# A mixture-of-experts trunk: expert outputs added to the tokens by TensorE, block turns on VectorE

## What is computed

```python
expert_id = g_sel[:, None] * EXPERTS_PER_GROUP + top_i     # top-1 group, top-2 experts in it
...
def expert_block(args):
    xb, e = args
    hid = jax.nn.silu(xb @ w1[e]) * (xb @ w3[e])
    return hid @ w2[e]

ys = lax.map(expert_block, (xs, block_e)).reshape(n_rows, D)
ys = ys * w_buf[:, None].astype(ys.dtype)
out = jnp.zeros((T + 1, D), ys.dtype).at[tok_buf].add(ys)[:T]
```

## Time and profile before

| | us |
|---|---|
| median of 3 runs (lowest, highest) | 1711.97 (1709.97, 1712.51) |
| the profiled execution's own time | 1715.51 |
| its span, from the first to the last instruction | 1713.8 |

### The profile page before, as it was taken

How to read it: one execution, slowest core, us unless ns; L and a number is a source line. 1 busy time by engine, 2 the same in 40 slices (tenths; PEclk the granted TensorE clock), 3 DMA queues, 4 the chain that set the end, 5 groups by cost and what they waited for, 6 DMA issues and landing times.

```text
span 1713.8 us, 39713 instructions
## 1 busy us (share of the span) xinstructions
PE 1489.0 (87%) x16229; PEld 1002.4 (58%) x16230; DVE 588.4 (34%) x1383; ACT 342.5 (20%) x669; POOL 38.5 (2%) x68
## 2 busy tenths in 40 slices
PE   8999999997997999864999989989989999866673
PEld 7888888654554555532887844468555556433342
DVE  5347632422221222213634356733222222211113
ACT  5441313200000000001432334524100000000000
POOL 3000000000000000002000000000000000000001
PEclk9999999999999999987998999989999999988887
DMA  5621226799999999998212122055999997999995
GB/s 203 221 98 56 93 97 245 284 420 423 425 421 423 421 424 421 421 422 335 75 51 99 50 98 75 25 196 220 368 422 424 423 411 312 401 418 422 421 421 180
DMA packets 100998, 487.04 MB, mean 284 GB/s; under 512 B 10736, under 2 KB 22896, under 8 KB 84304
## 3 DMA queue, kind: packets, MB, share of 16 engines
q1 hardware_dynamic: 76544, 457.19, 65.5%
q10 hardware_dynamic: 20528, 17.10, 3.1%
q0 software_dynamic: 3872, 11.98, 2.2%
HBM read 467.58 MB, written 18.64 MB: 284 GB/s over the span
## 4 chain that ended last, share of the span: by engine, by line
issue 51%; DMA 24%; PE 21%; DVE 1%; ACTq 1%; POOL 1%; SPq 0%; POOLq 0%; ACT 0%; DVEq 0%
DMA EB<-in_m_w 17%; DMA y_rows<-SCR 5%; PE ps L1174 5%; PE ps L1176 5%; PE ps L1175 5%; PE ps L1304 2%; ACTq L623 1%; PE ps L1384 1%; DMA EB<-y_rows,pos_i 1%; PE ps L1319 1%; PE ps L1286 1%; DVE X L939 1%; POOL EB L484 1%; PE ps L1170 0%; DMA gain<-in_a_norm 0%
## 5 line engine op out<-in xcount | busy, mean ns | idle before, releaser
L1304 PE MATMUL ps<-EB,SCR 128*32 128x256 f32 x6016 | 386.9, 414 | 119.8 <-DMA EB<-in_m_w 93.2
L1304 PEld LDWEIGHTS ps<-EB,SCR 128*32 128x32 f32 x6016 | 221.5, 119 | 277.6 <-issue 191.7
L896 DVE TENSOR_TENSOR SCR<-SCR,ps 64x256 f32<-64x256 f32 x94 | 39.7, 423 | 616.1 <-ACT SCR L611 616.1
L1176 PE MATMUL ps<-EB_r 128*128 128x512 f32 x512 | 201.0, 393 | 0.0
L1319 PE MATMUL ps<-EB,SCR 128*32 128x256 f32 x3008 | 184.0, 385 | 1.3 <-issue 0.3
L1286 PE MATMUL ps<-H,SCR 128*32 128x256 f32 x3072 | 184.3, 379 | 0.0
L616 ACT ACTIVATE SCR<-ps 128x256 f32 (+1 forms) x94 | 36.1, 384 | 560.1 <-issue 374.6
L1286 PEld LDWEIGHTS ps<-H,SCR 128*32 128x32 f32 x3072 | 107.3, 110 | 58.2
L1319 PEld LDWEIGHTS ps<-EB,SCR 128*32 128x32 f32 x3008 | 105.6, 110 | 53.5 <-issue 18.4
L1174 PE MATMUL ps<-EB_r,H_r 128*128 128x512 f32 x320 | 127.4, 398 | 1.0 <-DVE EB L972 1.0
L1175 PE MATMUL ps<-EB_r,H_r 128*128 128x512 f32 x320 | 125.4, 392 | 0.0
(11 more groups left out here) (218 smaller groups left out, 1389.9 us busy)
## 6 DMA issues: line engine op xcount, KB each, us to landing
EB<-in_m_w SPq DMA_DIRECT2D x192, 2048.0 KB, 10.1
EB<-in_a_w_in SPq DMA_DIRECT2D x8, 2048.0 KB, 9.4
y_rows<-SCR ACTq DMA_DIRECT2D x376, 32.0 KB, 5.9
EB<-in_a_w_out SPq DMA_DIRECT2D x4, 2048.0 KB, 7.7
EB<-in_kv_w SPq DMA_DIRECT2D x4, 2048.0 KB, 14.2
EB<-in_b_w_qg SPq DMA_DIRECT2D x4, 2048.0 KB, 8.0
y_rows<-X SPq DMA_DIRECT2D x2, 2048.0 KB, 15.9
SCR<-ncum_rows ACTq DMA_DIRECT2D x16, 256.0 KB, 3.7
```

Source lines behind the costliest of these rows:

```text
L896: v.tensor_tensor(hid[0:HALF, :], silu[HALF:P, :], ps[0][HALF:P, 0:CW], ALU.mult).then_inc(m["hid"], 1)
L1176: return mm(o, left[1], right[0], start=False, stop=stop)
L1304: last = mm(ps[0][g * CAP:(g + 1) * CAP, 0:CW], xT[:, k, :], w[:, k, g % 2 * CW:(g % 2 + 1) * CW], start=k == 0, stop=k == KD - 1)
```

## The change

`y_rows`, its stores, `gather_outputs` and `combine` are gone. In their place:

- ACT copies the down products of item n, times the weight of each slot (`slot_w`), into `y_parts` as fp32r; DVE writes the rest (exact value minus the rounded one) as a second fp32r part. Two items are kept.
- `spread_tokens` on DVE builds 0/1 matrices of 32 x 256 for each of the four partition groups, from the rows of positions `pos_row`: which of 256 tokens each slot of two items belongs to.
- `move` on PE multiplies these with `y_parts`: 32 products of 32 rows of contraction, 128 tokens and 256 columns of output, in the four row groups of the array, each group into its own PSUM bank. In iteration n it handles the items n-1 and n-2 and one half of the tokens (`n & 1`), and it stands behind `gather(n + 1)`. DVE then adds two blocks of 1024 columns to `X`. After the loop two more `move`s handle what is left.
- The transposes of `hid` and of the gathered rows are gone from PE: DVE turns them in blocks of 32 x 32 (`v.transpose`), for which w1 and w3 are read with other columns side by side, and the rows of w2 are laid out as `(p c) n` instead of `(c p) n`.
- Before the loop there are new steps: the rows of positions by PE (8 products), `slot_hot` and `item_hot` on DVE, `slot_w` by PE (32 products) and ACT.
- The start of the keys and values of layer 0 is reordered: the split of its first weight tile now stands among the norms of the blocks.

The diff, cut to its core:

```diff
@@ moe_act @@
-                act.wait_ge(y_filled, 16 * ((Y_ROWS - SLOTS) // T))
-                item_silu(0)
-                item_output(0)
-                with act.Fori(1, total) as n:
-                    item_silu(n)
-                    store_before(n)
-                    item_output(n)
-                store_before(total)
...
+                act.wait_ge(slot_w_done, 2 * l + 1)
+                a.activation(slot_w, ps[6][:, 0:MAX_ITEMS], ACT.Copy).then_inc(slot_w_done, 1)
+                act.wait_ge(slot_w_done, 2 * l + 2)
+                with act.Fori(0, total) as n:
                     act.wait_ge(m["up"], n + 1)
+                    a.activation(silu, ps[0][:, 0:P], ACT.Silu).then_inc(m["silu"], 1)
                     act.wait_ge(m["down"], n + 1)
+                    a.activation(y_parts[:, bass.ds(n & 1, 1), 0, :], ps[2][:, CW:2 * CW].unsqueeze(1), ACT.Copy,
+                                 scale=slot_w[:, bass.ds(n, 1)]).then_inc(m["y_hi"], 1)
@@ moe_dve @@
+                def turn_item(n):
+                    dve.wait_ge(m["gath"], n + 1)
+                    v.transpose(xg.rearrange("p k c -> p (k c)"), ps[1][:, 0:CW]).then_inc(m["xg"], 1)
+                    dve.wait_ge(m["xg"], n + 1)
+                    v.tensor_tensor(xT, xg, gpk[:, l, :].unsqueeze(2).to_broadcast([P, KD, CAP]), ALU.mult)\
+                        .then_inc(m["xT"], 1)
+
+                def spread_tokens(dst, which, items, link, ready):
+                    toks = [pos_row[:, k, bass.ds(which * 2 * P, 2 * P)] for k in range(2)]
+                    for i in range(2):
+                        link(v.tensor_scalar(dst[:, i, :], toks[0], item_slot[:, bass.ds(items[i] + 2, 1)], None,
+                                             ALU.is_equal), i)
+                    for i in range(2):
+                        v.scalar_tensor_tensor(dst[:, i, :], toks[1], item_slot[:, bass.ds(items[i] + 2, 1)],
+                                               dst[:, i, :].bitcast(F32), ALU.is_equal, ALU.add).then_inc(ready, 1)
...
                 with dve.Fori(0, total) as n:
                     dve.wait_ge(m["silu"], n + 1)
-                    v.tensor_tensor(hid[0:HALF, :], silu[HALF:P, :], ps[0][HALF:P, 0:CW], ALU.mult).then_inc(m["hid"], 1)
-                    item_rows(n + 1)
-                    dve.wait_ge(m["hidT_tr"], n + 1)
-                    v.tensor_copy(hidT.rearrange("p (h j) c -> p j h c", h=2),
-                                  ps[2][:, 0:2 * P].rearrange("p (j c) -> p j c", j=2)[:, :, 0:HALF]
-                                  .rearrange("p j (h c) -> p j h c", h=2)).then_inc(m["hidT"], 1)
-                    item_xT(n + 1)
+                    v.tensor_tensor(hid.rearrange("p (c r) -> p r c", c=KE), silu.rearrange("p (r c) -> p r c", c=KE),
+                                    ps[0][:, P:2 * P].rearrange("p (r c) -> p r c", c=KE), ALU.mult).then_inc(m["hid"], 1)
+                    dve.wait_ge(m["hid"], n + 1)
+                    v.transpose(hidT.rearrange("p k c -> p (k c)"), hid).then_inc(m["hidT"], 1)
+                    turn_item(n + 1)
+                    dve.wait_ge(m["moved"], n + 1)
+                    for t in range(2):
+                        X_t = X[:, bass.ds((n & 1) * 2 + t, 1), :].rearrange("p a (g n) -> p (a g) n", g=CG)
+                        add = v.tensor_tensor(X_t, X_t, moved[1][:, :, t, :], ALU.add)
+                    add.then_inc(m["added"], 1)
...
+                    spread_tokens(spread, (n + 1) & 1, (n - 1 + ((n + 1) & 1), n - 1 + (n & 1)),
+                                  lambda ins, i: link(ins, i + 1), m["spread"])
+
+                    dve.wait_ge(m["y_hi"], n + 2)
+                    v.scalar_tensor_tensor(y_parts[:, bass.ds(n & 1, 1), 1, :], ps[2][:, CW:2 * CW].unsqueeze(1),
+                                           slot_w[:, bass.ds(n, 1)], y_parts[:, bass.ds(n & 1, 1), 0, :].bitcast(F32),
+                                           ALU.mult, ALU.subtract).then_inc(m["y_lo"], 1)
+                    select(n + 2, m, 0, lambda ins, k: link(ins, k + 2))
+                spread_tokens(spread, 1, (total - (total & 1), total - 2 + ((total + 1) & 1)), lambda ins, i: then(ins),
+                              end_spread)
@@ moe_pe @@
+                def move(banks, sides):
+                    for t in range(2):
+                        for i in range(2):
+                            for k in range(2):
+                                for g in range(CG):
+                                    rows = slice(g * CAP, (g + 1) * CAP)
+                                    last = mm(moved[banks][:, g, t, :], sides[rows, i, t * P:(t + 1) * P],
+                                              y_parts[rows, i, k, :], start=i == 0 and k == 0, stop=i == 1 and k == 1)
...
                         last.then_inc(m["up"], 1)
                         gather(n + 1)
-                        pe.wait_ge(m["hid"], n + 1)
-                        for j in range(2):
-                            last = nc.tensor.transpose(ps[2][:, j * P:(j + 1) * P], hid[:, j * P:(j + 1) * P], ident[:, :])
-                        last.then_inc(m["hidT_tr"], 1)
-                        transpose_item(n + 1)
+                        move_items(n)
                         pe.wait_ge(m["hidT"], n + 1)
                         pe.wait_ge(m["w2"][s], 16 * loads)
...
+                pe.wait_ge(m["y_lo"], total + 1)
+                pe.wait_ge(end_spread, 4 * l + 2)
+                move(1, spread_end).then_inc(end_moved, 1)
+                pe.wait_ge(end_spread, 4 * l + 4)
+                move(0, spread).then_inc(end_moved, 1)
@@ after moe_dve @@
+            def add_moved(l, t):
+                dve.wait_ge(end_moved, 2 * l + t // 2 + 1)
+                X_t = X[:, t, :].rearrange("p (g n) -> p g n", g=CG)
+                v.tensor_tensor(X_t, X_t, moved[1 - t // 2][:, :, t % 2, :], ALU.add).then_inc(x_moe, 1)
```

323 lines of the change are left out of this document (177 added, 146 removed).

## The result

| | before | after |
|---|---|---|
| median, us | 1712.24 (1709.97 to 1713.45, 4 runs) | 1666.81 (1663.28 to 1670.87, 4 runs) |
| profiled execution, us | 1715.5, span 1713.8 | 1670.87, span 1669.1 |
| ratio | | 0.9737, interval 0.9712 to 0.9762 |

What follows compares the result with a forecast made beforehand. DMA engines bound most of the mixtures, PE some stretches, and the two ends wait on stores and fetches. Items and loads +5, ends -26: -21 on the profiled 1715.5 gives 1694.5; the median lies 3.5 lower, so 1691 us, range 1670 to 1738.

Steps and rivals of the forecast that it cites:

- The loads: Weight loads where DMA is full: 0.3 us less per expert without stores, -6 us in layer 0, -4 in layer 1.
- The layout: New layout of w2 changes the packets of its loads: 0, bounds plus and minus 0.2 us per load.
- The items: Longer items where PE gates loads: +0.55 us inside an expert, +0.27 at a change; +5 us layer 0, +9.2 layer 1.
- the front of layer 1: New steps before layer 1's item loop, on PE ahead of the first item: about 2.7 us.
- The period: Time between starts of successive items' up products on PE: 8.6 us inside an expert, 9.0 and 9.55 at changes.
- The ends: After each layer's last item, no fetches to wait for: -13.8 us in layer 1, -13.1 and +1 in layer 0, together -26.
- B: Rival: the move's products on PE run in series, 3.9 us a move, total 1839 us; chance 0.08.
- C: Rival: DVE's chain from move to `select` makes the item cycle 9.6 us instead of 8.6, total 1731 us; chance 0.27.
- D: Rival: items cost nothing, an 8.2 us cycle, and loads gain their full 0.5 us; total 1672 us; chance 0.10.
- the sum: All terms: +5 for items and loads, -26 for both ends, -21 us in total, forecast 1691 us.
- the ring: Per-item PE and DVE cycle: gather, move, adds, spread, low part, `select`, hand-overs; 8.6 us, bounds 8.2 and 9.8.

Runs made afterwards that it cites:

- e11: Changed kernel with the items' stores put back and w2 in the old layout, w1 and w3 columns read by a strided view: 1696.68 us, ratio 0.9907.
- e8: Changed kernel with w2 in the old layout, w1 and w3 columns read by a strided view, nothing left out: 1678.92 us, ratio 0.9779.
- e4: Changed kernel with the four stores of each item put back on ScalarE's queue, with their waits, w2 in the new layout: 1733.99 us, ratio 1.0109.
- e2: Kernel before without the items' stores, y_rows filled once early; only its layer 0 is read: 1677.25 us, ratio 0.9778.
- e7: Changed kernel with all 32 products of each move in one row group of TensorE: 1928.31 us, ratio 1.1243.
- e5: Changed kernel with VectorE's `select` placed ahead of the wait for the move and the adds: 1657.78 us, ratio 0.966.
- e13: Changed kernel with four stores an item of the same size and place, from a buffer nobody overwrites and without waits: 1682.34 us, ratio 0.9809.

## Why the prediction was off

**The loads, the term that failed.** "I take 0.3 per expert where DMA is the bound ... 20 loads in layer 0, -6; 14 in layer 1, -4. The new layout of w2 changes its packets; 0." Counted by kernels with equal items, from e11 to e8 the stores are worth 0.9907 - 0.9779, or 22 us, and from e8 to the changed kernel the layout 0.9779 - 0.9737, or 7 us: 29 where 10 were forecast. Three slips make it:

- The number of items. 0.3 us is what the working had for the stores of one item, and it charged that once for an expert, which has 1.5 items on average. In layer 0 TensorE holds loads up in the 19th to 22nd interval; these four take 62.8 us in e11 and 62.7 in e8. The other 24 intervals hold 38 items and fall by 12.5 us, from 15.42 to 14.90 each: 0.52 us a load, but 0.33 an item. In the last 12 intervals of layer 1, with 13 items, it is 0.31 an item (15.22 to 14.89). The kernel before has 15.30 there. So the price of an item was nearly right, between the 0.3 by bytes and the 0.41 that the working had from the share of engine time, and the number of items was left out.
- The number of loads. It was charged to 20 and 14 of the 28. From e11 to e8 the loads fall by 12.6 us in layer 0, over those 24 intervals, and by 8.9 in layer 1, where every part gains: the first ten intervals 2.8 us, the six around the held-up loads 2.1, the last twelve 4.0.
- The layout. At 0 with a bound of 0.2, it is 0.23 a load, beyond its bound.

The split into 22 and 7 holds for this order, stores first. With the stores in place the new layout costs 35 us (e11 to e4, 0.9907 to 1.0109), and taking the stores out then brings 64; only the sum, 29, is free of the order. The prediction put no price on ScalarE's wait for a landing, which the layout makes longer. That did no harm only because the change drops the stores, and the wait with them.

**The items.** This term was nearly right, in part by luck: at the new pace of the loads TensorE holds them up 5.7 us more in each layer, and the front of layer 1 takes 1.5, together 12.9 against 14.2. Half of it exists only because the loads are quicker: with the stores on both sides, before and e11, the loads differ by +2.5 and +3.7 us, and without them, e2 and e8, by +2.4 in layer 0. The period was right to 0.05 us inside an expert; at an ordinary change it is 8.65 and not 9.0, and a loop turn is 9.84, not 9.55.

**The ends.** -13.0 against -13.8, and -11.9 (-13.5 from the last silu) against -12. Here the working holds step by step. The first product of the projection, and the last adds of layer 1, beside the earlier trace rows:

```profile
797.11 4.90 PE L1198 MATMUL ps<-tri_in,tri 128*128 128x128 f32 x24
801.77 0.47 PE L1202 MATMUL ps<-EB_r,H_r 128*128 128x512 f32 x1
```

```profile
1660.90 4.62 DVE L937 TENSOR_TENSOR X<-X,ps 128x1024 f32<-128x1024 f32 x4
```

Behind the last up products at 1646.54 the adds end 19.0 us later; 18.7 were forecast.

**The front and the attention.** The first item of layer 0 starts 2.1 us later, but the first w1 there is issued at 337.80 as at 337.79 before, so that this is hidden, as said. The projection's first groups are 2.5 us longer, because the turns of blocks 2 and 3 now wait inside them. Some 2 us more in the attention are within the scatter of 4 us between executions; no cause is claimed for them.

**The rivals.** B is refuted by the 1.22 us of the move and by e7. Its price, 1839, was also too low: the real one is 1928. It let the granted clock fall only after waits, and the slower down products behind a move alone are 75 of the 89 us. C is refuted by VectorE's 5.25 us. D, at 1672, came nearest, for half the reason: the loads gain, and more than its 0.5 us each, but the items are not free, as e5 shows by making them cheaper. The rule of the Trainium skill, "TensorE: Matmul & The Clock Gate", section "LDWEIGHTS (loading the stationary operand)", gave an estimate of 3.4 us for the 32 loads in a row. The trace of the changed kernel does not agree with that as the cost of four row groups: the whole move takes 1.22 us. It agrees with Part 3, "The mechanism", of the same page of the Trainium skill, by which loads overlap running products where row groups differ. With one row group (e7) the weight loads are busy for 3.87 of the 4.00 us, near the estimate. The move takes 4.1 us there, so four groups give 3.4 times the rate. The Trainium skill, same page, section "Measured speedup vs the span model", reports 3.07 times for products of 512 columns, where these have 256.

By the experiments as a whole: everything but stores and layout brings 1 - 0.9907, or 16 us, where the sum had 11; the stores then bring 22 and the layout 7, where it had 10 and 0.

## What to carry to other kernels

Price a transfer beside full DMA engines, and count how often it happens per load: here the price of an item was right and the number of items was missing. Ask separately who waits for its landing: stores of the same bytes cost 12 to 16 us when nobody waited and 64 to 67 when ScalarE did, and the same layout of the loads made the kernel slower with the stores and their wait in it and faster without them. In a ring of hand-overs, write down which operations lie side by side: taking `select` off the ring was worth 9 to 13 us, while exchanging the gather and the move was worth nothing, since it put the move on the ring and took `select` off.

## What the hardware showed that I had not expected

- The granted clock fell behind a stretch in which TensorE was busy without a pause, but in one row group only: 1.00 during 4.00 us of the move in e7, then 0.54 over the next 3.20 us, and so 53 times, always late in a move or just behind it. In the changed kernel, with the products in four groups, it is 1.00 between 600 and 700 us, a stretch full of such items. That the single row group is the cause is likely but not shown: e7 also makes the move three times as long.
- Pieces of 16 KB rather than 4 KB shorten a load of 6.3 MB by 0.23 us (14.91 to 14.68) and lengthen the landing of a 32 KB store on another queue from 5.9 to 6.6 us.
- 92 stores of 128 KB and 368 of 32 KB cost the loads of layer 0 the same: 427.9 us in either.
- The group rows of the page show 94 loads of an activation table, one an item, where the kernel before has 2 at its silu. They are hidden: ScalarE is idle for at least 1.4 us more in front of every silu. The scaled copy of the output does not bring them, since e4, e11 and e13 have the same copy and again 2 loads; in these, as in the kernel before, the first item stands ahead of the loop.

```profile
L621 ACT ACT_TABLE_LOAD x94 | 120.6, 1283 | 2.0 <-ACT SCR L617 0.3
```
